# Seven block products for eight in the square output products, and compressed keys' attention in block-diagonal tiles with queries turned in pairs

## The reference

```
x = x + (g_a * (o_a @ w_branch_a) + g_b * (...) + g_c * (...)) @ w_out      # first block: 256x1024 by 1024x1024

# each of two layers
mix = concat(mla(...), nsa(...))                 # 8 latent heads of 64, 8 sparse heads of 64
x = layer_norm(ALPHA * x + mix @ w_out_2)        # ALPHA = 4 ** 0.25
o = cross_attention(x @ xa_wq_2, memory @ xa_wkv_2)
x = layer_norm(ALPHA * x + o @ xa_wo_2)
x = layer_norm(ALPHA * x + conv_ffn(x))

# in nsa: 15 compressed keys and values for each of 2 groups of 4 heads
kc, vc = compress(k_cmp), compress(v_cmp)        # (15, 2, 64): gelu(flat @ w1 + b1) @ w2
s = q @ kc * scale - slope * (t - end)           # 8 heads of 64, 15 keys
o = sigmoid(gate) * (masked_softmax(s) @ vc) + selected and window branches
```

## Time and profile before

| what | value |
| --- | --- |
| runs of the kernel before | 1807.29, 1794.82, 1807.10 us; median 1807.1 |
| the profiled execution | 1795.17 us, span 1793.4 us |
| granted TensorE clock, mean over the span | 0.997 |
| PE busy | 1727.9 us, 96% |
| DVE busy | 1127.3 us, 63% |
| ACT busy | 358.8 us, 20% |
| POOL busy | 202.9 us, 11% |
| read from HBM | 262.56 MB |

### The profile page before, as it was taken

How to read it: one execution, slowest core, us unless ns; L and a number is a source line. 1 busy time by engine, 2 the same in 40 slices (tenths; PEclk the granted TensorE clock), 3 DMA queues, 4 the chain that set the end, 5 groups by cost and what they waited for, 6 DMA issues and landing times.

```text
span 1793.4 us, 22877 instructions
## 1 busy us (share of the span) xinstructions
PE 1727.9 (96%) x8822; PEld 1309.5 (73%) x8822; DVE 1127.3 (63%) x2159; ACT 358.8 (20%) x884; POOL 202.9 (11%) x131
## 2 busy tenths in 40 slices
PE   7999999999999999999999999999999999999997
PEld 5887478877748885477784869984668767599953
DVE  6776467966655876642272549996712653479985
ACT  1111000034411110202261112220121530222210
POOL 1221211120101212120001000002110000000020
PEclk9999999999999999999999999999999999999999
DMA  9644454514256544536305335544356105165440
GB/s 317 217 149 143 163 188 159 188 48 156 89 165 212 187 155 150 181 102 210 139 6 166 104 118 188 175 155 164 131 139 220 54 2 210 47 212 188 148 159 23
DMA packets 162505, 265.63 MB, mean 148 GB/s; under 512 B 4008, under 2 KB 105684, under 8 KB 162270
## 3 DMA queue, kind: packets, MB, share of 16 engines
q1 hardware_dynamic: 157470, 248.18, 41.1%
q0 software_dynamic: 4768, 15.48, 2.6%
q10 hardware_dynamic: 160, 0.52, 0.1%
HBM read 262.56 MB, written 1.08 MB: 147 GB/s over the span
## 4 chain that ended last, share of the span: by engine, by line
PE 76%; DVE 15%; DVEq 4%; ACT 2%; issue 2%; DMA 1%; SPq 1%; ACTq 0%
PE psum L786 15%; PE psum L946 12%; PE psum L842 10%; PE psum L759 8%; PE psum L898 5%; PE psum L1064 3%; PE psum L1147 3%; PE psum L1347 3%; PE psum L1390 3%; PE psum L1099 3%; DVE work L2509 3%; PE psum L997 2%; DVE ring L1941 2%; PE psum L749 2%; PE psum L884 2%
## 5 line engine op out<-in xcount | busy, mean ns | idle before, releaser
L631 POOL TENSOR_TENSOR work<-ring,work 128x1024 f32<-128x1024 f32 (+1 forms) x57 | 141.4, 2481 | 806.5 <-DVE work L1943 806.5
L946 PE MATMUL psum<-ring,work 128*128 128x512 f32 x352 | 161.1, 593 | 3.5 <-DVE work L2473 3.5
L1939 DVE TENSOR_TENSOR work<-ring 128x1024 f32<-128x1024 f32 (+1 forms) x90 | 110.8, 1232 | 80.3 <-PE psum L946 77.6
L759 PE MATMUL psum<-ring,x_t 128*128 128x512 f32 x320 | 140.0, 595 | 7.4 <-ACT x_t L1444 7.4
L946 PEld LDWEIGHTS psum<-ring,work 128*128 128x128 f32 x352 | 66.3, 190 | 85.1 <-issue 79.9
L946 PE MATMUL psum<-work 128*128 128x512 f32 x264 | 122.5, 592 | 0.0
L759 PEld LDWEIGHTS psum<-ring,x_t 128*128 128x128 f32 x320 | 60.0, 190 | 81.5 <-issue 71.8
L1941 DVE TENSOR_TENSOR ring<-ring 128x1024 f32<-128x1024 f32 (+1 forms) x92 | 113.3, 1232 | 6.8
L1943 DVE TENSOR_TENSOR work<-ring 128x1024 f32<-128x1024 f32 (+1 forms) x90 | 108.2, 1202 | 6.7
L898 PE MATMUL psum<-x_t,ring 128*128 128x128 f32 x832 | 98.0, 276 | 6.9 <-ACT x_t L1444 6.9
L898 PE MATMUL psum<-x_t,work 128*128 128x128 f32 x832 | 101.4, 275 | 0.0
(11 more groups left out here) (265 smaller groups left out, 2833.8 us busy)
## 6 DMA issues: line engine op xcount, KB each, us to landing
ring<-in_ffn_w_up_dram SPq DMA_DIRECT2D x66, 1024.0 KB, 7.8
ring<-in_w_in_dram SPq DMA_DIRECT2D x21, 2048.0 KB, 7.9
ring<-in_ffn_w_down_dram SPq DMA_DIRECT2D x20, 2048.0 KB, 7.9
ring<-in_ffn_w_gate_dram SPq DMA_DIRECT2D x22, 1024.0 KB, 5.4
ring<-in_xa_wkv_dram SPq DMA_DIRECT2D x8, 2048.0 KB, 7.9
ring<-in_w_out_dram SPq DMA_DIRECT2D x6, 2048.0 KB, 8.8
ring<-in_xa_wq_dram SPq DMA_DIRECT2D x4, 2048.0 KB, 7.8
ring<-in_xa_wo_dram SPq DMA_DIRECT2D x4, 2048.0 KB, 9.9
```

The source lines that it names most:

```text
L631: nc.gpsimd.tensor_tensor(t4, quarters(n, chunks, pitch)[2], t2, ALU.subtract).then_inc(fourth_ready, 1)
L759: return mm(bank(banks[2 * i + h]), acts[:, c, i * P:(i + 1) * P], ring[:, (n0 + c // 4) % RING, o:o + 512], start=(c == 0), stop=(c == KD ...
L946: last = mm(sums[p], acts[p][:, q, :], rhs[:, i, :], start=(q == 0), stop=(q == KF // 2 - 1))
L1939: v.tensor_tensor(t3, b22, b12, ALU.subtract)
```

## The change

**Square products.** residual_product goes and shared_product takes its place: seven products of quarter size, each over four pairs of 128 rows, 28 matmul calls of 512 columns for 32, into banks 0, 1, 2, 3, 6, 7, and again 1. Its order: turn tile 0, product 1, half of product 2, turn tile 1, the rest of 2, then 6, 5, 3, 7, 4. It waits for DVE's weight sums ahead of 6, for two of the activation sums ahead of 6 and all four ahead of 3, and ahead of 4 for POOL's fourth sums (share_fourth) and for DVE's addition of product 2, whose bank 4 takes over (share_in). Behind L_OUT, PE waits for DVE's addition of product 7 ahead of the second memory values, which use its bank.

DVE adds the seven banks in shared_in, like gathered: 1 to four blocks, 2 to one, 6 to three, 5 to two, 3 to one, then tile 0's norm, then 7 to two and 4 to one, then tile 1's norm. It makes the activation sums when tile 1 has been turned (act_sums_of), then the weight sums of the next stage (as before two panels behind OUT1, one in the layers), then these additions. The weight sums for the square products themselves stand at new places: for OUT1 behind the head norms and between the mixing steps, for L_OUT as six single steps ahead of units 9, 11, 13, 15, 17 and 19 of the layers' attention, for L_WO in the query projection behind panel 0's first additions. POOL makes t4 in place of b21 in the ring, after product 2 (share_done).

**Compressed keys.** Queries are turned in pairs of heads, 128 columns at a time: two batches for four. Keys for S and W units are turned two groups at a time, one batch for two, and two DMAs on ACT's queue copy them to the other halves of the partitions. The compressed keys stand in a block-diagonal tile KBD (two heads, 30 columns), the hidden values are spread over 32-row strips (HPAD), and the compressed values stand in a block-diagonal VBD. Kind K then has four products of 30 columns, two transposes of 128 columns and two products of 256 columns, and DVE fills 128x256 with zeros ahead of its logits. POOL's fills change accordingly, and one more waits for comp_in.

```diff
@@ PE: the square products
-            def residual_product(n0, acts, banks, turn_tile, l=None):
...
+            def shared_product(n0, f0, a0, turn_tile, l=None):
+                n0 = at(n0, N_LAYER, l)
+                k = OUT_FORMS.index(f0)
+                acts = stationary(XT, XS[0:3], 0)
+
+                def product(p, d):
+                    rhs = moving(f0 + d, n0 + d, 4, D)[p]
+                    for i in range(2):
+                        q = 2 * d + i
+                        last = mm(share_bank(p), acts[p][:, q, :], rhs[:, i, :], start=(q == 0), stop=(q == KD // 2 - 1))
+                    return last
+
+                turn_tile(0)
+                arrived(n0)
+                product(1, 0)
+                product(2, 0)
+                arrived(n0 + 1)
+                product(1, 1).then_inc(share_done, 1)
+                turn_tile(1)
+                product(2, 1).then_inc(share_done, 1)
+                pe.wait_ge(forms_ready, f0 + 2)
+                pe.wait_ge(acts_ready, a0 + 1)
+                product(6, 0)
+                product(6, 1).then_inc(share_done, 1)
+                product(5, 0)
+                product(5, 1).then_inc(share_done, 1)
+                pe.wait_ge(acts_ready, a0 + 2)
+                product(3, 0)
+                product(3, 1).then_inc(share_done, 1)
+                product(7, 0)
+                product(7, 1).then_inc(share_done, 1)
+                pe.wait_ge(share_fourth, 2 * k + 2)
+                pe.wait_ge(share_in, 2 * k + 1)
+                product(4, 0).then_inc(panel_done, 1)
+                product(4, 1).then_inc(panel_done, 1)
@@ PE: behind the layers' first square product
+                pe.wait_ge(share_in, 4 * l + 4)
                 memory_values(1, (0, 1), (6, 7))
@@ PE: kind K
-                    return [(QTN[0:HD, s, q], kcT[:, s // 4, :])]
+                    return [(QTN[:, s, q], KBD[:, 30 * (s // 2):30 * (s // 2) + 30])]
...
-                    return vc[:, s // 4, :]
+                    return VBD[:, s, :]
@@ PE: batches of queries
-                for j in range(4):
-                    turn_columns(j, [D_NQ + (2 * j + s) * HD for s in range(2)])
+                for j in range(2):
+                    batch(E_NSA + j, [P2[:, i, D_NQ + m * P:D_NQ + (m + 1) * P] for m in (2 * j, 2 * j + 1) for i in range(TT)], l)
@@ PE: compressed keys and values
                 mm(PO[0:HD, 0:30], w2k, hidden[:, 0:30], start=True, stop=True)
+                mm(PO[:, 64:94], small[:, 0:P], hidden[:, 0:30], start=True, stop=True)
@@ POOL: fourth sums
                     pool.wait_ge(forms_ready, f + 1)
+                    if f in OF_OUTS:
+                        chunks, pitch = 4, D
+                        pool.wait_ge(share_done, 6 * (OF_OUTS.index(f) // 2) + 2)
@@ DVE: additions
+                def tile_in(i):
+                    if i == 0:
+                        add(1, quads)
+                        dr()
+                        add(2, quads[:, 0:1, :]).then_inc(share_in, 1)
+                        add(6, quads[:, 1:4, :])
+                        dr()
+                        add(5, quads[:, 1::2, :])
+                        dr()
+                        add(3, quads[:, 1:2, :])
+                    else:
+                        add(7, quads[:, 2:4, :]).then_inc(share_in, 1)
+                        dr()
+                        add(4, quads[:, 2:3, :])
@@ DVE: first block
+            act_sums_of(B_Y + 4)
             weight_sums(F_UP2, KD, 512)
             weight_sums(F_UP2 + 1, KD, 512)
-            rms_rows(8, 2, both_halves(residual(P_OUT1 + 1, 1, (0, 1, 2, 3), 1.0, 1.0)))
+            rms_rows(8, 2, shared_in(P_OUT1, 0, 1.0))
@@ DVE: layers
-                attend(UNITS_2, U1, l)
+                out_steps = [step for d in range(2) for step in weight_sum_steps(F_LOUT + F_LAYER * l + d, 4, D)]
+                attend(UNITS_2, U1, l, {9 + 2 * x: step for x, step in enumerate(out_steps)})
                 both_tiles()
+                act_sums_of(at(E_O + 4, B_LAYER, l))
                 f0, c0 = F_LQ + F_LAYER * l, C_LQ + C_LAYER * l
                 weight_sums(f0, KD, 512)
-                layer_norm(15, gains_in(4, l), l, residual(L_OUT + 1, 2, (0, 1, 2, 3), 1.0, ALPHA, l))
...
+                layer_norm(15, gains_in(4, l), l, first_half(shared_in(L_OUT, 1 + 2 * l, ALPHA, l)))
...
                 for j in range(LQS):
                     combine_fourths = up_combined(j, c0, XQT[:, 4 * j:4 * j + 4, :])
+                    if j == 0:
+                        weight_sums(F_LWO + F_LAYER * l, 4, D)
+                        weight_sums(F_LWO + F_LAYER * l + 1, 4, D)
@@ DVE: kind K
-                        L3 = L[:, 0:120].rearrange("p (h n) -> p h n", h=8)
+                        v.memset(L[:, 0:T], 0.0)
+                        dr()
+                        L3 = L[:, 0:T].rearrange("p (h c) -> p h c", h=8)[:, :, 0:NC]
@@ ACT: the other halves of the keys
+                act.dma_start(KTN[HD:P, 5:12:4, :], KTN[0:HD, 4:12:4, :]).then_inc(key_shift, 16)
+                act.dma_start(KTN[0:HD, 6:12:4, :], KTN[HD:P, 7:12:4, :]).then_inc(key_shift, 16)
```

More of the change, by code:

```diff
@@ L1076, in turn @@
                     o = 0 if x["wide"] else (u % 2) * 512
-                    for s in range(1 if x["kind"] == "B" else x["subs"]):
+                    for s in range({"B": 1, "K": 2}.get(x["kind"], x["subs"])):
                         for kb in range(x["nk"]):
-                            c = s * x["keys"] + kb * P
-                            kw = min(P, x["keys"])
-                            last = nc.tensor.transpose(PT[0:kw, o:o + P], lbuf(x, u)[:, c:c + kw], ident)
+                            c = s * P if x["kind"] == "K" else s * x["keys"] + kb * P
+                            last = nc.tensor.transpose(PT[:, o:o + P], lbuf(x, u)[:, c:c + P], ident)
                             o += P
@@ L1091, in value @@
                     k = x["kind"]
[L1092 to L1093 removed]
+                    dv = P if k == "B" else T if k in "XK" else HD
+                    blocks = [(s, kb) for s in range({"B": 1, "K": 2}.get(k, x["subs"])) for kb in range(x["nk"])]
                     for n, (s, kb) in enumerate(blocks):
[L1095 removed]
+                        pt = PTS[:, u % 2, n * P:(n + 1) * P]
                         first = n == 0 if k == "A" else kb == 0
@@ L1518, in exps @@
                     elif x["kind"] == "K":
-                        activation(L[:, 0:120], L[:, 0:120], ACT.Exp).then_inc(probs_ready, 1)
+                        L3 = L[:, 0:T].rearrange("p (h c) -> p h c", h=8)[:, :, 0:NC]
+                        activation(L3, L3, ACT.Exp).then_inc(probs_ready, 1)
                     else:
@@ L1713, in _ @@
                     evacuate(L_UKV, H_UKV + j, lambda t: KV[:, t, 512 * j:512 * j + 512], 512, l)
-                for b in range(6, 8):
-                    turned_columns(b)
+                b = at(E_NSA + 4, B_LAYER, l)
+                act.wait_ge(turned, b + 1)
+                both_keys = bank(turn_bank(b)).rearrange("p (a b) -> p a b", a=2)
+                activation(KTN[0:HD, 4:12:4, :], both_keys[0:HD], ACT.Copy)
+                activation(KTN[HD:P, 7:12:4, :], both_keys[HD:P], ACT.Copy).then_inc(turned_out, 1)
+                act.wait_ge(turned_out, b + 1)
+                act.dma_start(KTN[HD:P, 5:12:4, :], KTN[0:HD, 4:12:4, :]).then_inc(key_shift, 16)
+                act.dma_start(KTN[0:HD, 6:12:4, :], KTN[HD:P, 7:12:4, :]).then_inc(key_shift, 16)
                 def projected(n, g, scale, dst):
@@ L1734, in _ @@
                 act.wait_ge(comp_out, at(1, 1, l))
-                copy(kcT, PO[0:HD, 0:30].rearrange("p (g n) -> p g n", g=2))
-                copy(vc, PO[0:NC, 512:640].rearrange("p (g n) -> p g n", g=2)).then_inc(comp_used, 1)
+                act.wait_ge(pads_zero, 6 + 2 * l)
+                in_pairs = KBD.rearrange("p (g s n) -> p g s n", g=2, s=2)
+                for s, o in ((0, 0), (1, 64)):
+                    r = slice(HD * s, HD * s + HD)
+                    copy(in_pairs[r, :, s, :], PO[r, o:o + 30].rearrange("p (g n) -> p g n", g=2))
+                for h in range(4):
+                    r = slice(32 * h, 32 * h + 32)
+                    last = copy(VBD[r, :, HD * h:HD * h + HD], PO[r, 512:640].rearrange("p (g e) -> p g e", g=2))
+                last.then_inc(comp_used, 1)
                 projected(L_WK[1], H_WK + 1, T ** -0.5, XK[1])
@@ L1887, in gathered, with act_sums_of @@
+            def act_sums_of(b_last):
+                dve.wait_ge(turned_out, b_last)
+                mid, last = act_sums(XT, XS[0:3], 0)
+                mid.then_inc(acts_ready, 1)
+                last.then_inc(acts_ready, 1)
             def gathered(k, scale_new, scale_old, l=None):
```

250 lines of the change are left out of this document (131 added, 119 removed).

## The result

The changed kernel takes 1822.0 us (median of 8 runs, 1817.8 to 1827.4), the kernel before 1806.9 (median of 8 runs beside them, 1794.8 to 1808.6). The ratio is 1.0107 with a 95% interval of 1.008 to 1.0133: slower by 1.1%, where 1827.8 us and 1.1% were forecast. (The quotient of these two medians is 1.0084, at the lower end of the interval; the text goes by the ratio.) The profiled execution took 1818.8 us, its span 1817.0 where that of before had 1793.4.

What follows compares the result with a forecast made beforehand. PE was taken to bound the output products, with DVE becoming the late one. First block +4.7 and +8.0 per layer made 20.7 us more: 1815.9 profiled, plus 11.9 to the median, 1827.8 us (1.1% slower), range 1797 to 1837.

Steps and rivals of the forecast that it cites:

- The order on DVE: Output products: from 6.86 us DVE does activation sums, weight sums, additions, norm; layers' first goes on at 33.0, not 29.6.
- PE waits for DVE again right behind it: Output products other than the layers' first: a slowed PE clock is not counted, as PE waits for DVE anyway.
- POOL's 4.3 us per stage: Each of five output products: POOL's two fourth sums hold up DVE's sums on SBUF operands by 4.3 us (3.5 to 4.6).
- POOL and DVE don't meet: Rival: POOL's sums find gaps and PE's rests stay near 3 us with no clock loss; 1801.4 us, chance 0.22.
- L_WO: Layers' second output product: PE's second panel comes at 40.95 us instead of 36.86, +4.1 per layer.
- The clock: PE rests from 26.1 to 33.0 in the layers' first product; regaining its clock costs 2.46 us per layer (0 to 5).
- Compressed keys: Layers' compressed keys' attention: fewer score, turn and value instructions on PE's path save 5.26 us per layer over two tiles.
- Batches: Two of ten transposing batches go: no wait for ACT's copy (0.60), last two not made (1.11), -1.75 us per layer.
- The six steps: Weight sums inside the layers' attention: 3.8 us at units 9 to 13, 1.0 at 15, 0 from 17; +4.8 per layer.
- all steps exposed: Rival: all six weight-sum steps in the attention cost time, 7.6 us instead of 4.8 a layer; 1833.4 us, chance 0.15.
- The level: From the profiled execution's forecast, 1815.9 us, to the median of the runs: 11.9 us added, giving 1827.8.
- It does what it says: Rival: DVE keeps up everywhere and the savings on PE hold, -31.1 us, 1776.0 us; chance 0.09.

Runs made afterwards that it cites:

- Experiment two: Changed kernel with DVE's next-stage weight sums ahead of its activation sums at the five products, OUT1's second set behind the norms: ratio 0.9918 to the kernel before.
- experiment one: Changed kernel with POOL's two fourth sums made after a square product's fourth block product instead of its second: ratio 1.0036 to the kernel before.
- the squares alone: Kernel before with only the square products' part of the change, compressed keys as they were: ratio 1.0207 to the kernel before.
- experiment eight: Changed kernel with 7 matmuls that nobody reads put in PE's wait ahead of the second memory values: ratio 1.0074 to the kernel before.
- experiment three: Changed kernel with L_OUT's six weight-sum steps taken out of the layers' attention and put ahead of it: ratio 1.0053 to the kernel before.
- both mended: Changed kernel with weight sums ahead of activation sums and the six weight-sum steps ahead of the attention: 1779.8 us, ratio 0.9859 to the kernel before.
- seven: Changed kernel with 13 matmuls that nobody reads put in PE's wait ahead of the second memory values: ratio 1.0131 to the kernel before.
- the keys alone: Kernel before with only the compressed keys' part of the change, square products as they were: ratio 0.9911 to the kernel before.

## Why the prediction was right, and where its terms were off

The sign, the size and the mechanism held. By its own steps:

- **The order on DVE** (the start at 6.86, then activation sums, weight sums, additions, norm). L_OUT goes on at 32.81 us, forecast 33.0; OUT1's second panel comes at 41.17, forecast 41.2, and DVE's additions there begin at 24.01, forecast 24.0. Experiment two shows that the order is the cause: changed alone, it brings 34 us, POOL's company included. One wait was missing from PE's own schedule: at OUT1 product 4 waits for the addition of product 2 (which by the forecast's own numbers ends at 27.0) and began at 27.2, not 22.6. Behind that wait it ran at half clock, 6.19 us instead of 3.60. It changed nothing, since DVE was still in the first tile's norm when it ended, as the step "PE waits for DVE again right behind it" says.
- **POOL's 4.3 us per stage**, bound by 3.5 and 4.6: 2.1 and 2.0 us, 4.1 in all, at each place that I read, and experiment one moves it with POOL. The Trainium skill ("SBUF — State Buffer", Who interferes with whom) says that the order of issue decides who blocks. The rows agree, one sum at a time. In layer 0 the ends come in turn: POOL at 952.66, DVE at 953.74, POOL at 955.96, DVE at 957.04, each 1.1 us (DVE) or 2.2 us (POOL) behind the other engine's end, a little under what such a sum takes alone (1.23 and 2.34). These times are what comes out if each sum is held until the one issued before it on the other engine has ended. As both engines had a next sum ready, both paid: POOL's two took 6.2 us instead of 4.68, DVE's two 6.6 instead of 2.5. The rival "POOL and DVE don't meet" is out.
- **L_WO** was mis-sized: +4.1 forecast, +4.8 measured. The step that failed is the one in the part on the clock, "in the other stages PE waits for DVE again right behind it", so that a slow clock costs nothing there. The first panel behind L_WO took 6.54 us instead of 3.84, PE then turned the second tile late, and only 2 of the 2.7 us were hidden. Two other executions fit this: with first panels of 5.45 and 5.36 us the second one came at 40.83 and 40.82 us (the squares alone and experiment eight, layer 0), close to the 40.95 of the forecast.
- **The clock**, 2.46 us once per layer, measured 1.84 and 1.92 (3.6 in both layers by experiment eight). The mechanism is shown by experiment eight. The size is not a fixed one: behind waits of 6.6 to 7.0 us at the same place the stage took 1.51 and 2.90 us more in experiment three and 2.94 and 2.72 with the squares alone, so that the 2.46, taken from a rest of 10 us, lies inside what was seen, and that it came within 0.6 us is no proof of the way it was worked out.
- **Compressed keys**: -5.26 forecast, -5.5 by experiment three. The wait for ScalarE's copy of the memory keys (L1779, 1.03 us) was there before but lay under 1.88 us of scores, and 0.81 no longer cover it all. The -5.5 holds that already.
- **Batches**: -1.75 forecast, -1.33 measured. The last batch (1.11) and one wait for a copy (0.60) did go from the chain. But 0.45 us of that wait had lain beside the batch ahead of it, of which the chain shows 0.84 us before (at 807.65) and 1.29 after (at 812.98).
- **The six steps** were the term most off: +4.8 forecast, +6.1 and +5.5 measured. The step that failed is "from 17 on ... two units of lead: 0". The chain shows the steps at 916.53 and 921.88 as links: each step holds up the logits of the unit behind it, and the forecast's own numbers say as much: one step of 1.27 us every two units, with 0.5 us free a unit, leaves DVE no lead. The rival "all steps exposed" (7.6) overstates it by the 1.5 to 2.1 us that were hidden.
- **The level.** I added 11.9 us to go from the profiled execution to the median, since the profile of before lay at the fast end of the runs. The changed kernel's profile lies 3.2 below its median. So this step is 8.7 us too high, while the sum of the stages, +20.7, is 2.9 below the 23.6 between the two spans; the time, 1827.8, is 5.8 above 1822.0 because the two errors cancel in part. That it came so near is to that extent luck. The mechanism does not rest on it.

"It does what it says" put the change at -31.1 us. With the two orders mended it brings -25 (0.9859 of 1802.6), so the other 6 are not had even then.

## What to carry to other kernels

When a fast scheme trades matmuls for sums on other engines, read when each sum can start and what stands ahead of it in that engine's program order; the same instructions in another order were worth 34 us here, twice what PE saves in all. Put sums of weights, which wait for no result, ahead of sums that do, and into an engine's rest ahead of a stage and not between the links of a chain that it paces. And give GpSimd's work on SBUF operands a place beside VectorE's PSUM additions.

## What the hardware showed that I had not expected

A rest of PE costs twice: the wait and, behind it, 1.5 to 2.9 us on a 13.9 us block after 6.6 to 7.0 us of rest (six readings), and 1.5 to 2.7 us on a 3.84 us one after 4.0. A wait of 2.5 us at the same place cost 1.8 us behind it in layer 1 of experiment one and nothing in its layer 0. And a late stage with waits of only 1.13, 0.83 and 0.69 us and short batches between (PE busy 1.49 of 4.10 us) was followed by a panel at half clock (6.74 us in experiment one). The second cost is only paid where PE is what the rest waits for: in the attention and at OUT1's product 4 the clock fell to 0.50 as well, and no loss shows there.

The same code has the clock fall in one execution and not in another. In the turning and mixing ahead of the first block's product, which no experiment touches, PE's timeline has in the changed kernel and in the one with both mended:
```profile
479.10 1.09 PE L1056 MATMUL psum<-ident_flip,work 128*128 128x128 f32 x8 [0.81 <-DVE work L2242]
```
```profile
482.53 1.97 PE L1056 MATMUL psum<-ident_flip,work 128*128 128x128 f32 x8 [0.81 <-DVE work L2242]
```
The second ran at a granted clock of 0.60 to 0.68 around it and needed 31.89 us from the mixing's first product (485.18) to the first block's product instead of 30.22. Of the ten profiled executions six had the clock at 0.50 from 481 to 484 (experiments one, two, six, seven and eight, and the keys alone), and four had 1.00 (the kernel before, the changed one, experiment three and the squares alone). The stage of the memory keys takes 40.1 to 40.4 us in some and 41.7 to 43.7 in others. Such places are probably part of why one kernel's runs lie 10 to 14 us apart; that was not shown, and what decides it was not tried. So before the spans of two profiled executions are compared, these places have to be looked at: the one of the kernel before had neither.
